# Input projections by pieces of the contraction: chunks of 460 to 512 columns, five token tiles in open banks

## The reference

```python
mod = silu(cond) @ ada_w[i] + ada_b[i]          # 2 layers, 1024 x 6144 each
sh1, sc1, g1, sh2, sc2, g2 = split(mod, 6)
h = x * (1 + sc1) + sh1                         # 640 x 1024
z = h @ ev_w_in                                 # layer 0: 1024 x 4128
z = h @ od_w_in                                 # layer 1: 1024 x 3072
```

## Time and profile before

| | us |
|---|---|
| three runs | 1867.15, 1873.47, 1874.77 |
| median | 1873.47 |
| span of the profiled execution | 1869.1 |
| TensorE busy | 1512.7 |
| VectorE, ScalarE, GpSimd busy | 744.3, 427.0, 214.5 |

### The profile page before, as it was taken

The page is one execution under the profiler, slowest core; times in us unless marked ns, Lnnn a source line. Parts: engine busy times, 40 slices in busy tenths (PEclk is TensorE's granted clock), DMA queues, the critical chain, the costliest instruction groups (busy, mean ns, idle before and its releaser), DMA issues. The chain is left out here.

```text
span 1869.1 us, 25731 instructions
## 1 busy us (share of the span) xinstructions
PE 1512.7 (81%) x9767; PEld 1210.8 (65%) x9768; DVE 744.3 (40%) x1388; ACT 427.0 (23%) x832; POOL 214.5 (11%) x166
## 2 busy tenths in 40 slices
PE   2799999656899998499994199989997867999970
PEld 1688888546577445377883199987884446777760
DVE  0412122176477262311113835428993752111118
ACT  0312122142344111011112312125552111101113
POOL 1000000022000032100003500010000321100016
PEclk9899999878999899599997599999998877999995
DMA  7576754701000810559994032220005225877763
GB/s 253 180 233 219 235 194 159 171 12 31 1 1 1 264 65 23 166 206 320 354 354 184 23 94 69 75 63 2 1 1 182 101 90 192 282 262 252 268 217 145
DMA packets 190509, 277.82 MB, mean 149 GB/s; under 512 B 12888, under 2 KB 130352, under 8 KB 190416
## 3 DMA queue, kind: packets, MB, share of 16 engines
q1 hardware_dynamic: 180032, 239.15, 39.0%
q0 software_dynamic: 9520, 34.24, 5.2%
q10 hardware_dynamic: 864, 3.15, 0.4%
HBM read 246.90 MB, written 34.85 MB: 151 GB/s over the span
## 5 line engine op out<-in xcount | busy, mean ns | idle before, releaser
L479 PEld LDWEIGHTS psum<-in_parts 128*128 128x128 f32 x3360 | 410.2, 190 | 58.7 <-issue 58.7
L479 PE MATMUL psum<-in_parts 128*128 128x258 f32 (+1 forms) x3360 | 420.1, 286 | 24.7 <-PEq L324 24.7
L771 PE MATMUL psum<-layer 128*128 128x512 f32 x400 | 174.2, 595 | 2.7 <-PEq L697 2.7
L1775 PEld LDWEIGHTS psum<-layer 128*128 128x128 f32 x1280 | 145.7, 192 | 15.2 <-issue 7.7
L1775 PE MATMUL psum<-layer 128*128 128x128 f32 x1280 | 146.4, 275 | 6.7 <-DVE layer L1980 6.7
L1775 PEld LDWEIGHTS psum<-layer,arena 128*128 128x128 f32 x1152 | 136.3, 198 | 13.2 <-issue 6.7
L1775 PE MATMUL psum<-layer,arena 128*128 128x128 f32 x1152 | 137.0, 282 | 5.3 <-DVE layer L1980 3.7
L771 PEld LDWEIGHTS psum<-layer 128*128 128x128 f32 x400 | 75.9, 191 | 95.6 <-issue 94.1
L563 DVE COPY arena<-psum 128x258 f32<-128x258 f32 (+1 forms) x70 | 29.7, 425 | 238.5 <-PE psum L479 238.5
L1166 PE MATMUL psum<-layer 128*128 128x320 f32 (+1 forms) x384 | 114.1, 434 | 5.4 <-PEq L1356 2.1
L1263 ACT ACTIVATE layer<-psum,layer 128x640 f32<-128x640 f32 (+1 forms) x120 | 84.4, 707 | 118.7 <-DVE layer L1209 118.7
(11 more groups left out here) (298 smaller groups left out, 1870.5 us busy)
## 6 DMA issues: line engine op xcount, KB each, us to landing
arena<-in_moe_w SPq DMA_DIRECT2D x48, 1024.0 KB
layer<-in_moe_w SPq DMA_DIRECT2D x48, 1024.0 KB, 9.5
in<-in_ada_w SPq DMA_DIRECT2D x40, 1024.0 KB, 5.3
y_rows<-layer SPq DMA_DIRECT2D x64, 256.0 KB, 8.2
in<-in_ev_w_in SPq DMA_DIRECT2D x15, 1032.0 KB, 7.6
in<-in_od_w_in SPq DMA_DIRECT2D x11, 1024.0 KB, 5.2
start<-in_ada_w SPq DMA_DIRECT2D x8, 1024.0 KB, 16.5
arena<-mod_rows SPq DMA_DIRECT2D x16, 512.0 KB, 8.2
```

The costliest lines, as they stand in the source:

```text
L479: last = T.matmul(bank(g % W_BANKS)[:, 0:cw], a, b[:, k], start=(k == 0 and m == 0), stop=(k == KD - 1 and m == 2))
L771: last = T.matmul(bank(g % 4), feats[k][:, t * P:(t + 1) * P], wout[:, k, j * BANK:(j + 1) * BANK], start=(k == 0), stop=(k == kt - 1))
L1775: last = T.matmul(dst[:, (2 * f + m) * P:(2 * f + m + 1) * P], weights[m][:, k, f * P:(f + 1) * P], xT[:, k, :], start=(k == 0), stop=(k = ...
```

## The change

The contraction is cut. A `"w"` job is now a piece: 256 of the 1024 rows of the contraction (two of the eight k) by one chunk of columns, for all five token tiles. A chunk has 460 columns six times and 456 three times in layer 0 (9 chunks, 36 pieces), 512 columns in layer 1 (6 chunks, 24 pieces). A tile gets six matmuls in a piece; its bank stays open over the four pieces of a chunk, five banks at a time, and is copied out in the last one.

Weights move by pieces too. There are four slots for split pieces, three raw buffers with a semaphore each, and three pieces are split before a stream starts (`READY`), each with its own load, cast and subtraction in `modulated`. In the stream the parts of piece p + 3 are made at the job of piece p, as soon as the slot's last user is done (`used_w` counts finished pieces but the last of a chunk), and the load of piece p + 5 is issued there. Modulation halves follow the pieces: two behind each of the first four, one behind each of the others, the last one included. The rotation takes two views of 256 columns for each chunk, in the first two pieces of the next one. Buffers shift to other addresses. The diff, without context that stays, the addresses of other buffers and the renaming of semaphores:

```diff
-IN_CW = 258
-OD_CW = 256
-SPLIT = 2 * KD * TOK + 4 * KD * IN_CW
+IN_CW = 512
+EV_CUTS = [0] + [460 * n for n in range(1, 7)] + [2760 + 456 * n for n in range(1, 4)]
+OD_CUTS = [512 * n for n in range(7)]
+ROPE_CW = 256
+PK = 2
+NP = KD // PK
+SLOTS, RAWS, READY = 4, 3, 3
+PIECE = PK * IN_CW
+EV_PIECE = PK * 460
+SPLIT = 2 * KD * TOK + 2 * SLOTS * EV_PIECE
+OD_SPLIT = 2 * KD * TOK + 2 * SLOTS * PIECE
 ADA_CH = 6 * D // ADA_CW
...
-        W_FIRST = at(R - KD * IN_CW, KD * IN_CW)
-        def chunk_of_k(buf, cw):
-            return buf[:, 0:KD * cw].rearrange("p (k n) -> p k n", k=KD)
-        def w_part(w, n, cw):
-            return chunk_of_k(parts(2 * KD * TOK + (2 * (w % 2) + n) * KD * IN_CW, KD * IN_CW), cw)
-        def modulated(name, i, halves, sh, sc, w, cw):
+        def of_k(buf, cw):
+            return buf[:, 0:PK * cw].rearrange("p (k n) -> p k n", k=PK)
+        def first_piece(p, cw):
+            return of_k(at(R - (READY - p) * PK * cw, PK * cw), cw)
+        def w_part(p, n, size, cw):
+            return of_k(parts(2 * KD * TOK + (2 * (p % SLOTS) + n) * size, size), cw)
+        def w_source(w, p, c0, c1):
+            return w.rearrange("(k p) n -> p k n", p=P)[:, PK * p:PK * (p + 1), c0:c1]
+        def modulated(name, i, halves, sh, sc, w, cw, size):
...
-            first_in, first_high = sem(f"{name}_firstin"), sem(f"{name}_firsthigh")
+            first_in = [sem(f"{name}_firstin{p}") for p in range(READY)]
+            first_high = sem(f"{name}_firsthigh")
...
-                    sp.dma_start(chunk_of_k(W_FIRST, cw), w.rearrange("(k p) n -> p k n", p=P)[:, :, 0:cw]).then_inc(first_in, 16)
+                    for p in range(READY):
+                        sp.dma_start(first_piece(p, cw), w_source(w, p, 0, cw)).then_inc(first_in[p], 16)
...
-                        if k == 2:
-                            act.wait_ge(first_in, 16)
-                            A.copy(w_part(0, 0, cw), chunk_of_k(W_FIRST, cw)).then_inc(first_high, 1)
+                        if 2 <= k < 2 + READY:
+                            p = k - 2
+                            act.wait_ge(first_in[p], 16)
+                            A.copy(w_part(p, 0, size, cw), first_piece(p, cw)).then_inc(first_high, 1)
...
-                    pool.wait_ge(first_high, 1)
-                    nc.gpsimd.tensor_tensor(w_part(0, 1, cw), chunk_of_k(W_FIRST, cw), whole(w_part(0, 0, cw)), ALU.subtract)
+                    for p in range(READY):
+                        pool.wait_ge(first_high, p + 1)
+                        nc.gpsimd.tensor_tensor(w_part(p, 1, size, cw), first_piece(p, cw), whole(w_part(p, 0, size, cw)), ALU.subtract)
...
-            w_at = [n for n, j in enumerate(jobs) if j[0] == "w" and j[5][0] == 0]
...
+            pieces = [j for j in jobs if j[0] == "w"]
...
-            CB = KD * IN_CW
-            w_raw = at(R, CB)
+            w_raw = [at(R + b * size, size) for b in range(RAWS)] if pieces else []
...
-            def groups(job, first):
-                return [g for g in (NT * job[4] + t for t in job[5]) if g % 2 == first]
-            def next_chunk(n):
-                return [w + 1 for w in range(len(w_at) - 1) if w_at[w] == n]
+            def groups(p, which):
+                return [g for g in range(NT * (p // NP), NT * (p // NP + 1)) if g % 2 == which]
...
-                    def load_w(w):
-                        _, m, n0, cw, _, _ = jobs[w_at[w]]
-                        if w >= 2:
-                            sp.wait_ge(low, w - 1)
-                        sp.dma_start(chunk_of_k(w_raw, cw), m.rearrange("(k p) n -> p k n", p=P)[:, :, n0:n0 + cw]).then_inc(w_in, 16)
+                    def load_w(p):
+                        _, m, c0, c1, _ = pieces[p]
+                        if p >= READY + RAWS:
+                            sp.wait_ge(low, p - READY - RAWS + 1)
+                        sp.dma_start(of_k(w_raw[p % RAWS], c1 - c0), w_source(m, p % NP, c0, c1)).then_inc(w_in[p % RAWS], 16)
...
+                    for p in range(READY, min(READY + RAWS - 1, len(pieces))):
+                        load_w(p)
                     for n, job in enumerate(jobs):
                         if job[0] == "w":
-                            for w in next_chunk(n):
-                                load_w(w)
+                            if job[4] + READY + RAWS - 1 < len(pieces):
+                                load_w(job[4] + READY + RAWS - 1)
...
-                            _, _, _, cw, w, tiles = job
-                            if w:
-                                pe.wait_ge(high, w)
-                                pe.wait_ge(low, w)
-                            w_h, w_l = w_parts(w, cw)
-                            for t in tiles:
-                                g = NT * w + t
-                                if g >= W_BANKS:
+                            _, _, c0, c1, p = job
+                            cw = c1 - c0
+                            if p >= READY:
+                                pe.wait_ge(low, p - READY + 1)
+                            w_h, w_l = (w_part(p, n, size, cw) for n in range(2))
+                            for t in range(NT):
+                                g = NT * (p // NP) + t
+                                if g >= W_BANKS and p % NP == 0:
                                     pe.wait_ge((ev_a, ev_d)[g % 2], (g - W_BANKS) // 2 + 1)
-                                for k in range(KD):
-                                    x_h, x_l = (p[:, k, t * P:(t + 1) * P] for p in ht)
+                                for kk in range(PK):
+                                    k = PK * (p % NP) + kk
+                                    x_h, x_l = (part_[:, k, t * P:(t + 1) * P] for part_ in ht)
                                     for m, (a, b) in enumerate(((x_h, w_h), (x_h, w_l), (x_l, w_h))):
-                                        last = T.matmul(bank(g % W_BANKS)[:, 0:cw], a, b[:, k], start=(k == 0 and m == 0),
+                                        last = T.matmul(bank(g % W_BANKS)[:, 0:cw], a, b[:, kk], start=(k == 0 and m == 0),
                                                         stop=(k == KD - 1 and m == 2))
-                                last.then_inc(group, 1)
+                                if p % NP == NP - 1:
+                                    last.then_inc(group, 1)
+                            if p % NP < NP - 1:
+                                last.then_inc(used_w, 1)
...
-                def split_high(act, w):
-                    cw = jobs[w_at[w]][3]
-                    act.wait_ge(w_in, 16 * w)
-                    if w >= 2:
-                        act.wait_ge(group, NT * (w - 1))
-                    A.copy(w_parts(w, cw)[0], chunk_of_k(w_raw, cw)).then_inc(high, 1)
-                def split_low(dve, w):
-                    cw = jobs[w_at[w]][3]
-                    hi, lo = w_parts(w, cw)
-                    dve.wait_ge(high, w)
-                    V.tensor_tensor(lo, chunk_of_k(w_raw, cw), whole(hi), ALU.subtract).then_inc(low, 1)
+                def split_high(act, p):
+                    cw = pieces[p][3] - pieces[p][2]
+                    act.wait_ge(w_in[p % RAWS], 16 * ((p - READY) // RAWS + 1))
+                    if p >= SLOTS:
+                        w, kp = (p - SLOTS) // NP, (p - SLOTS) % NP
+                        if kp == NP - 1:
+                            act.wait_ge(group, NT * (w + 1))
+                        else:
+                            act.wait_ge(used_w, (NP - 1) * w + kp + 1)
+                    A.copy(w_part(p, 0, size, cw), of_k(w_raw[p % RAWS], cw)).then_inc(high, 1)
+                def split_low(dve, p):
+                    cw = pieces[p][3] - pieces[p][2]
+                    dve.wait_ge(high, p - READY + 1)
+                    V.tensor_tensor(w_part(p, 1, size, cw), of_k(w_raw[p % RAWS], cw), whole(w_part(p, 0, size, cw)), ALU.subtract).then_inc(low, 1)
...
-                            _, _, n0, cw, _, _ = job
-                            for w in next_chunk(n):
-                                split_high(act, w)
-                            for g in groups(job, 0):
-                                act.wait_ge(group, g + 1)
-                                A.copy(dst[:, g % NT, n0:n0 + cw], bank(g % W_BANKS)[:, 0:cw]).then_inc(ev_a, 1)
+                            _, _, c0, c1, p = job
+                            if p + READY < len(pieces):
+                                split_high(act, p + READY)
+                            if p % NP == NP - 1:
+                                for g in groups(p, 0):
+                                    act.wait_ge(group, g + 1)
+                                    A.copy(dst[:, g % NT, c0:c1], bank(g % W_BANKS)[:, 0:c1 - c0]).then_inc(ev_a, 1)
...
-                            _, _, n0, cw, _, _ = job
-                            for w in next_chunk(n):
-                                split_low(dve, w)
-                            for g in groups(job, 1):
```

(42 more changed lines are left out.)

14 lines of the change are left out of this document (6 added, 8 removed).

## The result

The changed kernel takes **1861.09 us** (median of 4 runs, 1859.79 to 1861.49) against 1871.35 for the kernel before on the same chip (median of 4): a ratio of 0.9946, 95% interval 0.9929 to 0.9964. It is 10.3 us faster, where 30.6 were forecast; the time lies 1.1 us above the range of 1831 to 1860, and within 1 us of the rival of a constant loss per matmul (1862). The profiled execution took 1859.79 us, its span is 1858.0.

What follows compares the result with a forecast made beforehand. TensorE's own instructions were taken to bound both projection stages, a zero-row store also ending the even one. Terms -17.6 (odd), -13.0 (even) and 0 (rest) sum to -30.6 us, from median 1873.47 to 1843 us; range 1831 to 1860.

Steps and rivals of the forecast that it cites:

- the rival of a constant loss per matmul: Both streams: each matmul loses a constant 13 ns at full clock; odd -9.8, even -2, 1862 us; chance 0.09.
- Three things say a floor: Projection matmuls: 13.3 ns lost at 256 columns is a short-matmul floor, by float32 matmuls, dense weight loads, 258-column cost.
- Odd layer: Odd stream: 1440 matmuls of 256 columns become 720 of 512 at 215.6 ns; -17.6 us, bounds -19.3 to 0.
- Even stream: Even layer to the zero store's issue: 460 columns at 194.0 ns, 456 at 192.3; next stage 13 us earlier.
- The other terms: Even stream: half clock +2.2, modulation halves 38.0, turns 9.5, job changes 6.5, start waits 2.8 us.
- The waits at the start: Even stream: TensorE waits 1.1 and 1.7 us for the first modulation halves; bounds 0.5 to 8.
- The split: VectorE and ScalarE in both streams: a piece's halves cost about 1 us each, under cover; cost nothing.
- Queue and transfers: Even stream: 460 KB piece takes 3.4 us; rival that the queue bounds the stage, 1906 us, chance 0.05.
- The fit of the Trainium skill: Weight transfers: 2.0 us plus bytes over 436 GB/s each; paid in turn, supply about 278 us, kernel about 1860.
- The granted clock: Start of both streams: half clock for 4.4 us (even) and 3.0 us (odd) as before; no fall within either.
- The zero store as the stage's end: Even stage: 5 MB zero-row store, not TensorE, sets its end; 4 us of TensorE's gain lost under it.
- The preparation: Before each stream: GpSimd subtracts three pieces in 6.1 or 6.7 us; 0 taken, 0.7 and 1.0 longer or 0.7 shorter.

Runs made afterwards that it cites:

- experiment 1: Changed kernel with the odd layer's chunks cut to ten widths from 64 to 512 columns; single execution, 1895.43 us.
- experiment 3: Changed kernel with the odd layer's activation and weight halves kept as bfloat16 instead of float32r; single execution, 1855.96 us.
- experiment 4: Changed kernel with 256-column chunks again in the odd layer, pieces and open banks kept; 1868.11 us, ratio 0.9978 to the kernel before.
- experiments 5, 6, 8 and 9: 5 MB zero store moved to ScalarE's queue (5: changed kernel, 1865.99 us; 6: kernel before, 1880.03) or inside the retention (8: changed kernel, 1851.3; 9: kernel before, 1868.92).
- experiment 7: Changed kernel with one piece split ahead instead of three; 1853.65 us, ratio 0.990 to the kernel before.

## Why the prediction was wrong

**The step that failed** is "Three things say a floor". The loss of 13.3 ns at 256 columns was measured rightly and read wrongly: it is a constant of each float32r matmul, 13.4 ns at 512 columns too (experiment 1, and the changed kernel itself). Of the three things, the float32 matmuls are of another type, and the type is what decides (experiment 3). The weight loads were nearly as dense as the matmuls, but the floor of the pair is 111 ns (experiment 1) and lies under the 120 that were measured. And that 258 columns cost what 256 do was read in a circle: the pause taken off was itself worked out from 120 ns a matmul. It happens to be true, 120.4 and 120.3 ns from start to start in that trace, but widths that are no multiple of 64 pay another constant (experiment 1: 260 less than 256), so it says nothing against one. None of the three was a measurement of a longer float32r matmul, and no row of before had one.

**Odd layer, -17.6 forecast, -9.1 measured.** 713 matmuls x (226.7 - 215.6) ns = 7.9 of the 8.5 us missing; the start at the half clock, forecast as 7 matmuls in 3.0 us, was 9 in 3.9, some 0.5 us more. The constant's rival said -9.8. That experiment 4, at the old width, is back at the old 175.7 us shows that the width alone made the gain of this stage.

**Even stream, -13.0 forecast, -0.7 measured.** 460 columns take 207.9 ns from start to start, 456 206.8, where 194.0 and 192.3 were put: 720 x 13.9 + 300 x 14.5 ns = 14.4 us up to the issue, more than the 12.3 missing. The other terms were thus some 2 us too dear. Here the rival (-2) was itself too kind, as these widths pay 16 to 17 ns and not 13. That its sum of 1862 comes within 1 us of the measured time is thus in part luck: the mechanism was right, but its two terms are 2.0 us too much, and 3.7 us from the preparations and the store, which it didn't have, stand against 2.6 of scatter.

**The waits at the start,** 1.1 and 1.7 forecast, 1.41 and 1.63 measured. **The split:** 1.16 us a half on VectorE for "about 1", no wait of TensorE for it. **Queue and transfers:** 460 KB landed in 3.6 us (3.4 by the line through two rows), at up to 371 GB/s beside full-clock matmuls; no wait beyond the two at the start, so halving the transfers cost nothing here, where they are queued one behind the other. The fit of the Trainium skill that the prediction weighed stands in another section of its page (DMA: Bandwidth & Descriptors, Anatomy of one DMA — SWDGE (gpsimd) path) and is one for transfers issued by GpSimd; these are issued by SyncE. **The bank, switched after every six matmuls:** the first of six comes after 226.5 ns, the others after 226.7. **The granted clock** rose from 0.50 to 1.00 3.5 us into the even stream and 3.9 into the odd one (4.4 and 3.0 before), and stayed up (0.99 over both).

**The zero store as the stage's end** was right, and experiments 5, 6, 8 and 9 show it. The stream's last sum ended 6.8 us earlier (355.1 to 348.3), the store was issued 2.7 earlier, of which 1.9 is the stream's earlier start: 4.1 us of the gain ended under it, where 4 were forecast. As the store then took 28.0 us for 29.5, the retention started 4.1 earlier, and 2.7 were lost in the end; why the store was quicker isn't known.

**The preparation** was put at 0 within +1.0 and -0.7, and gave -1.8, outside the bounds, and -0.5. GpSimd's three pieces took 7.47 and 8.13 us for the 6.1 and 6.7 forecast, and VectorE was held by each of them: its busy time rose by 0.3 and 1.0 us (14.32 to 14.64, 14.29 to 15.30). What got shorter is its wait for ScalarE, 2.10 us to 0.66 (experiment 7) in the even preparation, 2.20 to 0.75 in the odd one, a term that the prediction put at nothing. In the kernel before a cast of the whole chunk stood in front of the cast that VectorE waits for:
```profile
51.87 1.91 ACT L355 CAST in_parts<-arena 128x2064 fp32r<-128x2064 f32 x1 [0.39 <-DMA arena<-in_ev_w_in]
```
Now it is the cast of a piece, 0.96 us. The price of GpSimd's second and third piece (experiment 7: 5.9 us) was not seen.

The chances were too sure: 0.81 on a step that no row of the same type could carry, 0.09 on a rival against which only that circle stood.

## What to carry to other kernels

Before a pace is carried to another width, find two widths of the same type at the full clock; a loss seen at one width is a floor, a constant or a rate, and they differ by the whole gain. Where it is a constant, the gain is the number of instructions saved times that constant and no more: 13.4 ns for each of the 720 saved in the odd layer. And before an earlier end is counted, look at what else the next stage waits for: here one 5 MB store, last in its queue, kept the next stage waiting; moving it took 8.9 us off that stage, some 3 of them what it had hidden of TensorE's gain.

## What was not expected of the hardware

- A float32r matmul of 128 stationary columns costs its columns / 2.4 ns and 13.2 to 13.6 ns more at 256, 320, 384 and 512 columns, 15 to 19 at 456 to 500, 10.6 at 260; in bfloat16 2.5 at 512, 2.9 and 3.2 at 456 and 460. At the half clock the extra is gone (427 ns for 512). Why float32r has it stays open: it goes neither by stationary columns nor by contraction rows.
- The floor of such a pair of float32r weight load and matmul is 111 ns at the full clock (64 to 200 columns), 213 at the half (64 columns).
- 64 stationary columns shorten the load's record from 189 to 134 ns and make the matmul 3 ns dearer.
- A 5 MB store on one queue beside 1 MB loads on another made TensorE wait 14.7 us for one of the loads, which land in 5.7 (median) otherwise.
- A VectorE subtraction that starts beside one of GpSimd ends 0.7 us after it: 0.82 us alone, 2.23 beside one of 2.12, 4.64 beside one of 4.53.
